# Stick-breaking attention: the weighted values of two units run together every second step, and transposed weights return to their unit's buffer

## What is computed

```python
def stick_breaking_block(q, k, v, q_pos, k_pos):
    z = jnp.einsum('bqhd,bkhd->bhqk', q, k).astype(jnp.float32) * (HEAD_DIM ** -0.5)
    valid = k_pos[None, :] < q_pos[:, None]
    log_keep = jnp.where(valid, jax.nn.log_sigmoid(-z), 0.0)
    later = lax.cumsum(log_keep, axis=3, reverse=True) - log_keep
    a = jnp.where(valid, jnp.exp(jax.nn.log_sigmoid(z) + later), 0.0)
    return jnp.einsum('bhqk,bkhd->bqhd', a.astype(v.dtype), v)
```

## Time and profile before

| | us |
|---|---|
| median of 3 runs (2185.66 to 2186.67) | 2186.18 |
| span of the profiled execution | 2187.6 |
| PE busy | 2089.9 (96%) |
| DVE busy | 1616.3 (74%) |
| ACT busy | 1259.0 (58%) |
| POOL busy | 767.6 (35%) |

### The profile page before, as it was taken

How to read it: one execution, slowest core, us unless ns; L and a number is a source line. 1 busy time by engine, 2 the same in 40 slices (tenths; PEclk the granted TensorE clock), 3 DMA queues, 4 the chain that set the end, 5 groups by cost and what they waited for, 6 DMA issues and landing times. The chain is left out here.

```text
span 2187.6 us, 40169 instructions
## 1 busy us (share of the span) xinstructions
PE 2089.9 (96%) x13511; PEld 1763.6 (81%) x13512; DVE 1616.3 (74%) x2084; ACT 1259.0 (58%) x2199; POOL 767.6 (35%) x696
## 2 busy tenths in 40 slices
PE   8999999996899999899999897999999999999998
PEld 6888888885687887678787775888888888888887
DVE  3799999994777667867878868879699556466644
ACT  5322433344677677866676644768678456455533
POOL 1111444553566565645545453211111112111111
PEclk9999999996999999999999998999999999999999
DMA  7563334434333233433222116989899968667851
GB/s 227 190 205 136 120 126 155 133 107 144 108 123 110 80 111 102 115 100 116 80 73 93 54 71 247 377 309 370 299 369 373 305 205 279 216 208 264 286 165 35
DMA packets 211805, 393.17 MB, mean 180 GB/s; under 512 B 54781, under 2 KB 81789, under 8 KB 211677
## 3 DMA queue, kind: packets, MB, share of 16 engines
q1 hardware_dynamic: 198141, 357.42, 47.1%
q0 software_dynamic: 13536, 34.12, 6.6%
HBM read 315.42 MB, written 91.23 MB: 186 GB/s over the span
## 5 line engine op out<-in xcount | busy, mean ns | idle before, releaser
L2528 DVE TENSOR_TENSOR p_w_lo<-p_raw,p_w_hi 128x1024 fp32r<-128x1024 f32 (+1 forms) x196 | 330.3, 1718 | 134.2 <-ACT p_w_hi L2320 133.6
L2124 POOL TENSOR_TENSOR late<-late,p_past 128x1024 f32<-128x1024 f32 (+4 forms) x166 | 308.2, 1857 | 341.9 <-DVE p_past L1981 338.7
L796 DVE SCALAR_TENSOR_TENSOR p_ut<-p_ut,p_cw 128x512 f32<-128x512 f32 (+1 forms) x480 | 329.2, 760 | 0.0
L2320 ACT ACTIVATE p_w_hi<-p_raw 128x2048 fp32r<-128x2048 f32 (+1 forms) x150 | 271.6, 1842 | 62.1 <-PE p_up L2412 53.3
L1981 DVE TENSOR_TENSOR_SCAN p_past<-p_keep,p_past,p_one 128x513 f32<-128x513 f32 (+1 forms) x196 | 225.9, 1192 | 76.6 <-ACT p_keep L1798 74.6
L1798 ACT ACTIVATE p_keep<-p_zp 128x512 f32<-128x512 f32 (+3 forms) x326 | 158.8, 547 | 114.3 <-PE p_zp L1672 101.6
L2412 PE MATMUL p_gp<-p_w_hi,p_xt_hi 128*128 128x256 f32 x736 | 214.3, 291 | 0.0
L473 PE MATMUL p_pj<-p_w_hi,p_xt_hi 128*128 128x512 f32 x512 | 205.2, 401 | 4.2 <-DVE p_xt_lo L772 2.4
L2412 PE MATMUL p_gp<-p_w_lo,p_xt_hi 128*128 128x256 f32 x736 | 206.4, 280 | 0.0
L2412 PE MATMUL p_gp<-p_w_hi,p_xt_lo 128*128 128x256 f32 x736 | 206.4, 280 | 0.0
L473 PE MATMUL p_pj<-p_w_hi,p_xt_lo 128*128 128x512 f32 x512 | 200.6, 392 | 0.0
(11 more groups left out here) (315 smaller groups left out, 5005.2 us busy)
## 6 DMA issues: line engine op xcount, KB each, us to landing
p_raw<-in_w_up SPq DMA_DIRECT2D x96, 512.0 KB
p_raw<-in_w_gate SPq DMA_DIRECT2D x96, 512.0 KB
p_raw<-in_w_down SPq DMA_DIRECT2D x96, 512.0 KB
late<-in_w_up SPq DMA_DIRECT2D x32, 512.0 KB
late<-in_w_gate SPq DMA_DIRECT2D x32, 512.0 KB
late<-in_w_down SPq DMA_DIRECT2D x32, 512.0 KB
wide_raw<-in_w_in SPq DMA_DIRECT2D x56, 256.0 KB, 4.0
wide_raw<-in_x SPq DMA_DIRECT2D x17, 512.0 KB
```

What stands on the lines that cost most here:

```text
L796: dve.scalar_tensor_tensor(dst, src, cw[:, a, j:j + 1], dst, ALU.mult, ALU.add).then_inc(tap_done, 1)
L2124: pool.tensor_tensor(mine, mine, past_rows[:, u % NP, 0:n, 2:2 + w], ALU.mult).then_inc(a_done, 1)
L2320: act.activation(part(w_hi, p, wide), ring(n, wide), ACT.Copy).then_inc(whi_done, wide)
L2528: dve.tensor_tensor(part(w_lo, p, wide), ring(n, wide), part(w_hi, p, wide).bitcast(F32), ALU.subtract).then_inc(wlo_done, wide)
```

## The change

- V of two units of one tile and head group run one after the other in one step: the table `values_at` gives V(u) and V(u+1) to step u+5, where u is counted from the tile's first unit in twos. A tile's last unit keeps step u+4. So V runs in 84 steps, in 82 of them for two units, and 80 steps of the units' main run that had a V have none.
- The transposed copies go back into the unit's own half buffer, from which its transposes have just been read. `at` is gone, and its memory gives two more weight buffers (`wgt_rest`): NW = 6.
- The copies' wait on `av_done` is gone. The sigmoids' wait for a free buffer is now on V of unit u-6.
- Values tiles that replace old ones load one step later (`+ 5` for `+ 4`).
- What writes into `late` at the end waits for the last V (`av_done`) instead of the last transposes.

No matmul, copy or sigmoid is added or removed.

```diff
-        NW, NK, NP, NA, NZ = 4, 2, 3, 4, 2
+        NW, NK, NP, NZ = 6, 2, 3, 2
...
-        wgt = late.all.rearrange("p (n l) -> p n l", n=NW)
-        at = sb("at", [P, NA, 4 * P])
+        wgt_rest = sb("wgt_rest", [P, NW - LATE // UW, UW])
+        slots_of = [late.all[:, n * UW:(n + 1) * UW] for n in range(LATE // UW)]
+        slots_of += [wgt_rest[:, n, :] for n in range(NW - LATE // UW)]
...
+        values_at = {}
+        for i in last:
+            for u in range(first[i], last[i] + 1):
+                values_at.setdefault(min(u + (u - first[i] + 1) % 2, last[i]) + 4, []).append(u)
...
-                v_step[g, kt] = max(v_step[g, kt], user[old_key[g, kt]] + 4)
+                v_step[g, kt] = max(v_step[g, kt], user[old_key[g, kt]] + 5)
...
+        def weights_of(u, x, lo, hi):
+            return slots_of[u % NW][:, x * HW + lo:x * HW + hi]
...
-                if 0 <= s - 4 < len(units):
-                    values(s - 4)
+                for u in values_at.get(s, []):
+                    values(u)
...
                 if u >= NW:
-                    act.wait_ge(t_done, base[u - NW + 1])
+                    act.wait_ge(av_done, u - NW + 1)
...
-                if u >= 2:
-                    act.wait_ge(av_done, u - 1)
-                act.activation(at[:, n % NA, 0:w], tp[:, n % 2, 0:w], ACT.Copy).then_inc(cp_act, 1)
+                act.activation(weights_of(u, x, 0, w), tp[:, n % 2, 0:w], ACT.Copy).then_inc(cp_act, 1)
...
-                if u >= 2:
-                    dve.wait_ge(av_done, u - 1)
...
-                dve.wait_ge(t_done, base[end])
+                dve.wait_ge(av_done, end)
...
-                pool.wait_ge(t_done, base[end])
+                pool.wait_ge(av_done, end)
```

More of the change, by code:

```diff
@@ L1682, in transpose_weights @@
                         end = pe.transpose(tp[:, n % 2, b * P:(b + 1) * P],
-                                           wgt[:, u % NW, x * HW + b * P:x * HW + (b + 1) * P], ident[:, :])
+                                           weights_of(u, x, b * P, (b + 1) * P), ident[:, :])
                     end.then_inc(t_done, 1)
@@ L1701, in values @@
                                             v_sb[:, key_slot(g, kt), h * HD:(h + 1) * HD],
-                                            at[:, base[u] % NA, src:src + DEC],
+                                            weights_of(u, 0, src, src + DEC),
                                             start=(u == first[i] and b == 0 and h < PAIR),
@@ L1711, in values @@
                                         v_sb[:, key_slot(g, kt), h * HD:(h + 1) * HD],
-                                        at[:, (base[u] + x) % NA, b * P:(b + 1) * P],
+                                        weights_of(u, x, b * P, (b + 1) * P),
                                         start=(u == first[i] and b == 0), stop=(u == last[i] and b == hi - lo - 1),
@@ L1800, in sigmoids @@
                 if u >= NW:
-                    act.wait_ge(t_done, base[u - NW + 1])
+                    act.wait_ge(av_done, u - NW + 1)
                 for x in halves_in(u):
-                    act.activation(wgt[:, u % NW, x * HW:x * HW + w], zp[:, (base[u] + x) % NZ, 0:w], ACT.Sigmoid,
+                    act.activation(weights_of(u, x, 0, w), zp[:, (base[u] + x) % NZ, 0:w], ACT.Sigmoid,
                                    scale=SCALE).then_inc(sig_done, 1)
@@ L1991, in second_half @@
                 dve.wait_ge(t_done, n + 1)
-                if u >= 2:
-                    dve.wait_ge(av_done, u - 1)
-                dve.tensor_copy(at[:, n % NA, 0:w], tp[:, n % 2, 0:w]).then_inc(cp_dve, 1)
+                dve.tensor_copy(weights_of(u, half_count(units[u]) - 1, 0, w), tp[:, n % 2, 0:w]).then_inc(cp_dve, 1)
             def mean_squares(i):
@@ L2120, in product @@
                 n = half_count(units[u])
-                mine = wgt[:, u % NW, :].rearrange("p (x l) -> p x l", x=PAIR)[:, 0:n, 0:w]
+                mine = slots_of[u % NW].rearrange("p (x l) -> p x l", x=PAIR)[:, 0:n, 0:w]
                 pool.wait_ge(scan_done, u + 1)
```

## The result

The change makes the kernel slower: 2197.25 us (median of 8 runs, 2192.29 to 2201.60) against 2187.82 of the kernel before (8 runs on the same chip), ratio 1.0045 with the interval 1.0035 to 1.0055. That is 9.4 us where about none was forecast, and above the range's 2196.

A forecast was written before the change was run, and what follows sets the result against it. Attention was taken as bound by PE's stream plus its few waits; -28.7 + 20.3 + 16.4 - 7.8 - 3 + 1 + 2.3 = +0.5 on 2187.6, hence 2188.1, less 1.4 for the profiled execution: 2186.7 us, range 2177 to 2196.

The forecast's parts named there:

- The bound: Attention: its time is PE's stream plus few waits; PE is busy 96 to 99 us of every 100.
- The seam: PE's entry and exit around each group of weighted values (V): 0.35 us each, 82 saved by pairing, -28.7 us.
- The floor: In 39 steps that lose a V, the next scores must wait for ACT's sigmoid: +20.3 us.
- the banks: Behind steps that lose a V, 25 side jobs wait for banks that DVE or ACT must free: +16.4 us.
- Step 73: Example step losing its V: the sigmoid holds the next scores, so only 0.47 of 1.23 us is won.
- the wait of step 32: A "wo" job on PE waits 0.89 us for keys DVE moves out; removing V makes it longer.
- rival 1: Faster, at the side jobs: banks do not bind because DVE and ACT catch up; 2179 us, chance 0.28.
- Copies, loads, late waits: Moved waits and later values loads cost nothing; transposes waiting for copies cost +1 us (bounds 0 and 6).
- Rival 2: Slower, in the 39 short steps: transposes wait for ACT's copies, 6 us instead of 1; 2192 us, chance 0.24.
- rival 3: Inside a pair, the second V pays the same seam, so the 28.7 saving is absent; 2201 us, chance 0.03.
- The end: End of attention: `late` is released by the last V, so the last "mix" job waits longer on POOL: +2.3 us.
- the clock: PE's granted clock: longer waits could drop it; two drops of about 2 us each only at the range's edge.

The follow-up runs named there:

- e6: The change with 52 pairs, placed where neither sigmoid nor bank binds, instead of 82, against the kernel before: 2175.54 us, ratio 0.9947.
- e9: e6 with the memory `late` released two units earlier at the end of attention, against the kernel before: 2169.16 us, ratio 0.9912.
- e7: The change with only the 24 of its pairs whose empty step stands before a job waiting for its bank, against the kernel before: 2198.47 us, ratio 1.0049.
- e8: The change with only its other 58 pairs, without the 24 at waiting side jobs, against the kernel before: 2186.45 us, ratio 0.9989.
- e1: The change's buffers, copies and later release, but every V at its old step, against the kernel before: 2188.66 us, ratio 1.0004.
- e12: The whole change measured again in a second set of runs, against the kernel before: 2196.16 us, ratio 1.0035.
- e10: The change with its pairs at units 8, 27, 33, 39 and 102 taken apart, against the kernel before: 2188.84 us, ratio 1.0004.
- e11: The change's buffers with only the five pairs at units 8, 27, 33, 39 and 102, against the kernel before: 2200.59 us, ratio 1.0051.

## Why the prediction was wrong

**The bound: right.** Attention is PE's stream and its waits. Where the waits were kept away (e6, e9), 17.6 us came off between the first and the last scores, and some 17 (52 pairs at 0.35 or 0.26) were saved on PE.

**The seam: right in kind, 2.5 us too large.** 0.35 a group before scores, but 0.26 where a unit begins with its mask. I took all 82 from one kind of neighbour.

**The floor and the banks: right in place, in mechanism and, as far as a subtraction shows, in sum.** Step 73 won 0.47 as worked out, the wait of step 32 grew from 0.89 to 1.62, and the prices of single places gave the signs and sizes of e6, e7 and e8. From the first to the last scores +6.2 was measured; with about 26 saved at the seams and an estimated 5.3 of clock (below), 27 are left for the waits, and the sum had 26.9 (20.3 + 16.4 - 7.8 - 3 + 1). How they divide over the terms isn't shown. In rows, sigmoid waits grew by 8.0 and waits of side jobs by 8.3 (36.5 to 44.8, all rows of L1582 to L1634 together), less than the +20.3 and +8.6 of the sum. But each row leaves out some 0.2 us (the 0.73 at step 73 that reads 0.48), and there are 25 more waits for a sigmoid alone.

**The test I had named was a bad one.** "If PE's idle time grows by less than 20, rival 1 holds": it grew by 18.8 from the first to the last scores, and rival 1 (faster) was not what happened. PE's busy time there fell by only 12.6 where about 28 was forecast: the lower clock puts an estimated 5.3 back, and the part of each wait that its bracket leaves out is counted as busy. An idle total read from modelled ends is too small, by the more the more waits there are.

**Copies, loads, late waits: right.** e1 shows them at nothing; waits of T for a copy grew by 1.5 us in rows (1.8 to 3.3), where +1 was taken. Rival 2's time (2192) lies 5 us under what came and rival 3's (2201) 4 us above, but neither mechanism is the one that acted: the copies were waited for too little, and a second V directly behind the first did save its seam.

**The end: right**, +2.4 for +2.3.

**The step that failed is the one left out of the sum: the clock.** The prediction named further drops only beside rival 2, at about 2 us each and only as the edge of its range, and reasoned from 1.00 and 0.98 in two stretches. In the sum the clock stood at nothing. From the first to the last scores it forecast -1.8 in all, and +6.2 came. Half-clock time there rose by 10.7 us, an estimated 5.3 us of PE's work. The seam's 2.5 is the second piece; with these two the difference of 8.0 is covered to 0.2, though the split of the waits is not exact enough to make much of that.

Over all runs the clock went from .9832 to .9785 (.9794 in e12). Held against a span of 2190 that is 10.3 (8.5) us of a loss of 9.4 (7.7), but this takes all work at half clock as time lost one for one, and the runs say less. Among the runs of one kernel, time goes up by about 1.2 us for each .001 of clock (all kernels here together), not by 2.2; at that rate the clock is 5.6 (4.7) us of the loss. Compared at the same clock of .981, with few runs to go by, two of the change took 2192.5 us on average and one of e12 2194.7, two of the kernel before 2189.1: at an equal clock the change is still some 3 to 6 us slower, about what a sum of +0.5 with the seam's 2.5 put right would give. So the clock is the larger part of the miss, and not the whole of the loss.

And e10 and e11 show where most of the loss comes from: not from pairs as such, but from five places where the missing V lengthened a bank wait by 0.3 to 0.7 us. The sum had each of these waits at its length; the drops that can follow them it hadn't. That this second price was larger than the first is so in the mean clocks of e10 to e12; in e7, with the same five waits, the clock was lower by only .0017.

What the trace of the kernel before would have allowed: its own five drops all go with waits whose brackets read 2.5 to 3.2 us, and none follows the five waits of 0.7 to 1.15. Between 1.15 and 2 us it had one wait of 1.2 and one of 1.7, both without a drop, so nothing in it told that 1.4 to 1.9 are enough at times. That could have been a term with two ends, none of the five or all, at 1.7 us each (half of a drop of 3.4 us).

**Left open:** why one such wait is followed by a drop and the next is not; whether a wait's length, its neighbours or both decide; why the clock of e11 fell further than its five waits explain, and that of e7 less; what a lower mean clock costs, between 1.2 and 2.2 us for .001; the 1 us or so by which attention starts later in most of the other profiles (520.6 before; 520.3 to 522.1), and the few us by which the time behind attention differs from profile to profile (863.6 to 868.0).

## What to carry to other kernels

Moving work away from a place costs what that work had covered there: price each place by its own waits, and move only where there is room; the same edit gave +0.45% on every second step and -0.5% (with the end mended -0.9%) on 52 chosen ones. When a wait of TensorE grows, ask also what the clock does after it, and look at the granted clock of all runs, not only of the profile. Read waits from start to start, since a bracket counted from a modelled end leaves part of each one out.

## What the runs showed of the hardware

- TensorE's clock fell to 0.50 for 3.4 to 10.2 us after single waits whose brackets read 1.4 to 1.9 us, in 13 of 35 cases, in a stream that is otherwise some 92 to 94% busy, and in none of 35 where the same waits read 0.7 to 1.15. Of the longer ones (over 2.5 us from start to start, from 545 to 1300 us) a drop began during or right after 59 of 87. The Trainium skill ("TensorE: Matmul & The Clock Gate", A second HAM failure mode: psum-queue depth-cycling) tells of a kernel in which frequent short idle times between groups, as it cycles through PSUM banks, made the clock go back and forth. These waits for a bank are short too, and the runs agree that such idle times can bring the clock down; here single ones were enough.
- A group of 64-column matmuls between 128-column ones costs 0.35 us beside its own matmuls before scores of 384 or 512 columns, about 0.26 before a mask matmul of 128. From the start of the last transpose to the group's start it is 0.20, where a mask follows a transpose after 0.11 and a wide matmul after 0.03; from the start of the group's last record to the next matmul it is 0.20; and the first wide matmul behind the group takes 0.34, behind transposes 0.31. A second group directly behind the first adds only its matmuls (0.87 for 16 records), also when it reads other buffers.
- The four sigmoids of a unit on ACT in another order changed nothing that can be told, neither on the kernel before (0.9999) nor on the change (1.0033 against 1.0045 and 1.0035).
